# A two-layer decoder trunk: GLA outputs in four parallel banks with one root and one late reciprocal, and gate products in halves between the steps of sliding attention

## The reference, cut to what matters

```
h = rms_norm(x) * (1 + sc1) + sh1
gq, gk, gv, ga, gr, sq, sk, sv, mix_a, mix_b = split(h @ w_in)
y_gla = gla(gq, gk, gv, ga, gr) @ w_up_gla       # 4 heads, dk 64, dv 128, chunks of 64
y_swa = swa(sq, sk, sv) @ w_up_swa               # 8 heads of 64, window 128, 2 kv heads
merged = sigmoid(mix_a) * y_gla + sigmoid(mix_b) * y_swa
# gla, for each chunk n of each head:
#   o = tril(q_dec @ k_inv.T) @ v + q_dec @ state[n];  state[n+1] = decay[n] * state[n] + k_end.T @ v
#   out = o * (mean(o*o) + eps) ** -0.5 * gain * silu(r)
# swa, for each block n of 128 tokens, over blocks n-1 and n:
#   s = q @ k.T / 8, masked; p = exp(s - max) / (sum + exp(sink - max)); o = p @ v
```

## Time and profile before

| | us |
|---|---|
| median of 3 runs | 1620.25 (1618.32 to 1621.02) |
| the profiled execution, its own time | 1614.97 |
| its span (first to last instruction) | 1613.3 |
| PE busy | 1444.3 (90%) |
| DVE busy | 995.4 (62%) |
| ACT busy | 724.7 (45%) |
| POOL busy | 202.8 (13%) |
| mean granted TensorE clock | 0.943 |

### The profile page before, as it was taken

The page is one execution under the profiler, slowest core; times in us unless marked ns, Lnnn a source line. Parts: engine busy times, 40 slices in busy tenths (PEclk is TensorE's granted clock), DMA queues, the critical chain, the costliest instruction groups (busy, mean ns, idle before and its releaser), DMA issues.

```text
span 1613.3 us, 18635 instructions
## 1 busy us (share of the span) xinstructions
PE 1444.3 (90%) x7153; PEld 1140.3 (71%) x7154; DVE 995.4 (62%) x939; ACT 724.7 (45%) x776; POOL 202.8 (13%) x196
## 2 busy tenths in 40 slices
PE   4999967999998899999959997789998899999694
PEld 2766846666677788888748785678877778888472
DVE  2434365341656899999771746444358689999374
ACT  2425134322324677776542432432323567777160
POOL 1000000000001222233210000000002222332111
PEclk9999779999998999999979976999998999999897
DMA  9666200476765899999832210022257499999465
GB/s 304 234 224 237 79 1 6 162 251 224 252 225 199 292 348 391 395 398 398 307 119 104 102 56 0 1 95 73 94 190 271 158 358 380 392 393 392 170 221 188
DMA packets 152802, 350.24 MB, mean 217 GB/s; under 512 B 10511, under 2 KB 12755, under 8 KB 152723
## 3 DMA queue, kind: packets, MB, share of 16 engines
q1 hardware_dynamic: 140018, 312.77, 53.4%
q0 software_dynamic: 12704, 36.38, 6.3%
HBM read 334.43 MB, written 23.61 MB: 222 GB/s over the span
## 4 chain that ended last, share of the span: by engine, by line
PE 74%; DVE 12%; DMA 6%; issue 3%; DVEq 3%; ACT 2%; SPq 1%; POOL 0%; POOLq 0%; ACTq 0%
PE PS L1088 20%; PE PS L1090 19%; PE PS L1089 19%; PE PS L1022 3%; DMA ring<-in_w_ada 2%; DVE ring_parts L1959 2%; PE PS L1388 1%; PE PS L1200 1%; DMA ring<-in_w_down 1%; PE PS L1230 1%; DVEq L1726 1%; PE PS L1017 1%; DVE ring_parts L1605 1%; DVE reg L1766 1%; DVE reg L1746 1%
## 5 line engine op out<-in xcount | busy, mean ns | idle before, releaser
L1089 PE MATMUL PS<-ring_parts,reg_parts 128*128 128x512 f32 x768 | 300.1, 391 | 0.0
L1088 PE MATMUL PS<-ring_parts 128*128 128x512 f32 (+1 forms) x704 | 276.4, 393 | 11.8 <-DVE hT_parts L1613 5.7
L1959 DVE TENSOR_TENSOR ring_parts<-ring,reg_parts 128x2048 fp32r<-128x2048 f32 x124 | 277.9, 2283 | 2.6 <-ACT reg_parts L947 2.6
L947 ACT ACTIVATE reg_parts<-ring 128x2048 fp32r<-128x2048 f32 x124 | 230.4, 1909 | 63.2 <-DMA ring<-in_w_down 36.3
L1605 DVE TENSOR_TENSOR ring_parts<-ring,ring_parts 128x2048 fp32r<-128x2048 f32 (+1 forms) x52 | 112.8, 2210 | 168.3 <-ACT ring_parts L799 168.2
L1088 PE MATMUL PS<-reg_parts 128*128 128x512 f32 x504 | 202.0, 401 | 1.4 <-DVE reg_parts L1987 1.4
L1090 PE MATMUL PS<-reg_parts 128*128 128x512 f32 x504 | 196.9, 391 | 0.0
L1088 PEld LDWEIGHTS PS<-ring_parts 128*128 128x128 f32 x704 | 133.7, 190 | 66.9 <-issue 35.3
L1089 PEld LDWEIGHTS PS<-ring_parts,reg_parts 128*128 128x128 f32 x768 | 145.3, 189 | 28.6
L799 ACT ACTIVATE ring_parts<-ring 128x2048 fp32r<-128x2048 f32 (+1 forms) x52 | 93.3, 1844 | 159.7 <-DMA ring<-in_w_in 125.8
L1959 DVE TENSOR_TENSOR ring_parts<-ring,hT_parts 128x2048 fp32r<-128x2048 f32 x64 | 146.2, 2287 | 14.3 <-issue 13.2
(11 more groups left out here) (316 smaller groups left out, 2137.0 us busy)
## 6 DMA issues: line engine op xcount, KB each, us to landing
ring<-in_w_up SPq DMA_DIRECT2D x32, 2048.0 KB
ring<-in_w_gate SPq DMA_DIRECT2D x32, 2048.0 KB, 11.7
ring<-in_w_down SPq DMA_DIRECT2D x32, 2048.0 KB, 17.9
ring<-in_w_ada SPq DMA_DIRECT2D x40, 1024.0 KB, 5.5
ring<-in_w_in SPq DMA_DIRECT2D x16, 2048.0 KB, 8.1
ring<-in_w_ada SPq DMA_DIRECT2D x4, 2048.0 KB, 16.3
ring<-in_w_out SPq DMA_DIRECT2D x4, 2048.0 KB, 9.2
ring<-in_w_up_gla SPq DMA_DIRECT2D x2, 2048.0 KB
```

What stands on the lines that cost most here:

```text
L947: act.activation(w_high[part][:, cols], ring[:, 3 * k + part, cols], ACT.Copy).then_inc(w_hi[part], 1)
L1088: pe.matmul(out_, left[0], right[0], start=first, stop=False)
L1089: pe.matmul(out_, left[0], right[1], start=False, stop=False)
L1959: tt(ring_r[:, 3 * k + part, cols], ring[:, 3 * k + part, cols], w_high[part][:, cols].bitcast(F32), ALU.subtract).then_inc(w_lo[part], 1)
```

## The change

- `attm` becomes four tiles, one for each head; GpSimd clears the third and fourth, and DVE clears the first two as before. The causal scores come ahead of the chunk states' products, head by head as `r_done` rises. All masked scores are multiplied by v first, each head in its own bank 0 to 3 (the bank of its scores); then the state products follow, with the two heads of a pair taking turns.
- The sums of squares of the four heads are four products with 32 columns of ones into four partition groups of one bank. One root and one reciprocal of 128x512 serve all heads, and a product with one row of ones brings each head's row back to all partitions; DVE multiplies it into `rs` late (`norm_o`). The reciprocal stands on DVE between the scores' scaling of block 1 and the normalising of block 0.
- The transposes of q and k use banks 7, 5, 6, 7 and 5, 6; the scores of block 0 wait for `gate_o` (o times `rs`) only.
- Every gate product of `W_MA0` and `W_MA1` is issued in two halves of four chunks (12 instructions), at the places in the list below. DVE scales the scores of block n + 1, then normalises block n, and only then takes the maximum of n + 1. `split_low(W_MA1)` is taken in two halves, and `split_high(W_UPG)` on ACT comes earlier. GpSimd's router constants wait for the end of the new GLA norm.

The diff, cut; calls that stand alone on a line in the source are joined by semicolons:

```
-        attm = reg5[:, 0:2 * SEQ].rearrange("p (i t s) -> p i t s", i=2, t=NT)
+        attm = reg5[:, :].rearrange("p (h t s) -> p h t s", h=GH, t=NT)
-        osq = [reg0[:, 512 * h:512 * h + 512] for h in range(GH)]
-        orr = [reg7[:, 512 * i:512 * i + 512] for i in range(2)]
+        osq = [reg23[:, 512 * h:512 * h + 512] for h in range(GH)]
+        o_inv = reg7[:, 512:1024]
...
+    pool.wait_ge(b_done, at(b_done, l, 1))
+    pool.memset(attm[:, 2, :, :], 0.0).then_inc(scanm_made, 1)
+    if l == 0:
+        pool.wait_ge(ada_ready, 2)
+    pool.memset(attm[:, 3, :, :], 0.0).then_inc(scanm_made, 1)
...
+    act.activation(warm[:, :], one, ACT.Sqrt)
...
+    square_o(0); square_o(1); copy_qT(0); square_o(2); square_o(3)
+    act.wait_ge(ms_ready, at(ms_ready, l, 1))
+    act.activation(o_inv, PS[:, 4, :], ACT.Sqrt, scale=1.0 / P, bias=eps).then_inc(orr_done, 1)
+    for t in range(1, NT):
+        copy_qT(t)
...
+        copy_probs(3, b)
+    split_high(W_UPG)
+    act.wait_ge(o_done, at(o_done, l, 2 * GH + 1))
     act.activation(rs_parts[0].rearrange("p h s -> p (h s)"), reg4[:, :], ACT.Copy).then_inc(out_hi, 1)
+    copy_o(3)
...
+    for h in range(GH):
+        rows = slice(HD * (h % 2), HD * (h % 2) + HD)
+        pe.wait_ge(r_done, at(r_done, l, h + 1))
+        if h == 0:
+            pe.wait_ge(const_loaded, 16 * 9)
+        for t in range(NT):
+            mm = pe.matmul(PS[:, h, t * P:t * P + P], kinv[rows, h // 2, t * P:t * P + P],
+                           qdec[rows, h // 2, t * P:t * P + P], start=True, stop=True)
+        mm.then_inc(att_ready, 1)
+    pe.wait_ge(kt_done, at(kt_done, l, 2))
+    if l == 0:
         pe.wait_ge(ada_added, 2)
...
+        pe.wait_ge(att_done, at(att_done, l, h + 1))
+            pe.matmul(PS[:, h, t * P:t * P + P], v[:, t, h * P:h * P + P], attm[:, h, t, :],
+    pe.wait_ge(s_done, at(s_done, l, 1))
+    for m in range(2):
+            for h in (2 * m, 2 * m + 1):
+                rows = slice(HD * (h % 2), HD * (h % 2) + HD)
+                mm = pe.matmul(PS[:, h, n * CHUNK:n * CHUNK + CHUNK], S[rows, m, n, :],
+                               qdec[rows, m, n * CHUNK:n * CHUNK + CHUNK], start=False, stop=(n == NCH - 1),
+                               skip_group_check=True)
+                if n == NCH - 1:
+                    mm.then_inc(o_ready, 1)
+    pe.wait_ge(rope_done, at(rope_done, l, 1))
+    def transpose_q(t):
+        for a in range(QH // 2):
+            mm = pe.transpose(PS[:, QT_BANKS[t], a * P:a * P + P], qk[:, t, 2 * a:2 * a + 2, :].rearrange("p h d -> p (h d)"), ident[:, :])
+        mm.then_inc(qT_ready, 1)
+    for i in range(NT // 2):
+        for t in (2 * i, 2 * i + 1):
+            for g in range(KVH):
+                o = ((t % 2) * KVH + g) * P
+                mm = pe.transpose(PS[:, 5 + i, o:o + P], kd[:, t, g, :, :].rearrange("p r d -> p (r d)"), ident[:, :])
+        mm.then_inc(kT_ready, 1)
+    transpose_q(0)
+        mm = pe.matmul(PS[32 * h:32 * h + 32, 4, :], ones[:, 0:32], osq[h], start=True, stop=True, skip_group_check=True)
+    mm.then_inc(ms_ready, 1)
+    pe.wait_ge(kT_done, at(kT_done, l, 1))
+    transpose_q(1)
+    pe.wait_ge(kT_done, at(kT_done, l, 2))
+    transpose_q(2)
+    pe.wait_ge(qT_done, at(qT_done, l, 1))
+    transpose_q(3)
+    pe.wait_ge(o_done, at(o_done, l, GH))
...
+    def gate_half(bank, unit, j, part):
+        w = parts(unit)
+        for k in range(4 * part, 4 * part + 4):
+            mm = three_passes(PS[:, bank, :], [a[:, k, j * P:j * P + P] for a in w], [a[:, k, :] for a in hT_parts],
+                              k == 0, k == C - 1)
+        if part == 1:
+            mm.then_inc(mx_ready, 1)
+    def early_gate(n, part):
+        if part == 0:
+            if n == 0:
+                wait_unit(W_MA0)
+                pe.wait_ge(qT_done, at(qT_done, l, 2))
+            else:
+                pe.wait_ge(early_done, at(early_done, l, n))
+        gate_half(5, W_MA0, n, part)
+    def late_gate(j, part):
+        if j == 0 and part == 0:
+            wait_unit(W_MA1)
+            pe.wait_ge(sc_read, at(sc_read, l, NT))
+        elif j >= 2 and part == 0:
+            pe.wait_ge(o_done, at(o_done, l, INVERTED + j + 1))
+        gate_half(mix_bank(Q_MA1 + j), W_MA1, j, part)
...
+    def inverse_rows(h):
+        if h == 0:
+            pe.wait_ge(o_done, at(o_done, l, INVERTED))
+            pe.wait_ge(sc_read, at(sc_read, l, NT))
+        elif h >= 2:
+            pe.wait_ge(o_done, at(o_done, l, INVERTED + h - 1))
+        pe.matmul(PS[:, 2 + h % 2, :], ones[32 * h:32 * h + 1, :], o_inv[32 * h:32 * h + 1, :], start=True, stop=True).then_inc(ms_ready, 1)
 
...
+    scores(0); early_gate(0, 0); scores(1); early_gate(0, 1); transpose_probs(0, 1); early_gate(1, 0); values(0)
+    scores(2); early_gate(1, 1); transpose_probs(1, 0); transpose_probs(1, 1); early_gate(2, 0); values(1); scores(3)
+    early_gate(2, 1); transpose_probs(2, 0); transpose_probs(2, 1); early_gate(3, 0); values(2); early_gate(3, 1)
+    inverse_rows(0); inverse_rows(1); late_gate(0, 0); transpose_probs(3, 0); transpose_probs(3, 1); inverse_rows(2)
+    inverse_rows(3); late_gate(0, 1); values(3); late_gate(1, 0); late_gate(1, 1); next_half(0); late_gate(2, 0)
+    late_gate(2, 1); next_half(1); late_gate(3, 0); next_half(2); late_gate(3, 1); next_half(3)
...
+    split_low(W_MA1, parts_=(0,))
+    def gate_o(h):
+        tt(rs[:, h, :], PS[:, h, :], rs[:, h, :], ALU.mult).then_inc(o_done, 1)
+    def copy_kT(i):
+        dve.wait_ge(kT_ready, at(kT_ready, l, i + 1))
+        dve.tensor_copy(kT[:, :, 2 * P * i:2 * P * i + 2 * P].rearrange("p g (t s) -> p t g s", s=P),
+                        PS[:, 5 + i, :].rearrange("p (t g s) -> p t g s", t=2, g=KVH)).then_inc(kT_done, 1)
+    gate_o(0); gate_o(1); copy_kT(0); copy_kT(1); gate_o(2); gate_o(3)
...
+    def norm_o(h):
+        dve.wait_ge(ms_ready, at(ms_ready, l, h + 2))
+        tt(rs[:, h, :], PS[:, 2 + h % 2, :], rs[:, h, :], ALU.mult).then_inc(o_done, 1)
+    scale_scores(0); score_max(0)
+    dve.wait_ge(orr_done, at(orr_done, l, 1))
+    scale_scores(1)
+    dve.reciprocal(o_inv, o_inv).then_inc(o_done, 1)
+    normalise(0); score_max(1); copy_probs(0, 1); scale_scores(2); normalise(1); score_max(2); copy_probs(1, 0)
+    copy_probs(1, 1); scale_scores(3); normalise(2); score_max(3); copy_probs(2, 0); copy_probs(2, 1)
+    split_low(W_MA1, parts_=(1,))
+    normalise(3); norm_o(0); norm_o(1); copy_probs(3, 0); copy_probs(3, 1); norm_o(2); norm_o(3)
```

More of the change, by code:

```diff
@@ L1273, in next_half @@
                         condition_half(l + 1, j)
-                pe.wait_ge(pv_done, at(pv_done, l, NT))
-                wait_unit(W_MA1)
-                for j in range(C // 2):
-                    channel_major(mix_bank(Q_MA1 + j), W_MA1, slice(j * P, j * P + P)).then_inc(mx_ready, 1)
-                    next_half(j)
+                scores(0)
+                early_gate(0, 0)
+                scores(1)
+                early_gate(0, 1)
+                transpose_probs(0, 1)
+                early_gate(1, 0)
+                values(0)
+                scores(2)
+                early_gate(1, 1)
+                transpose_probs(1, 0)
+                transpose_probs(1, 1)
+                early_gate(2, 0)
+                values(1)
+                scores(3)
+                early_gate(2, 1)
+                transpose_probs(2, 0)
+                transpose_probs(2, 1)
+                early_gate(3, 0)
+                values(2)
+                early_gate(3, 1)
+                inverse_rows(0)
+                inverse_rows(1)
+                late_gate(0, 0)
+                transpose_probs(3, 0)
+                transpose_probs(3, 1)
+                inverse_rows(2)
+                inverse_rows(3)
+                late_gate(0, 1)
+                values(3)
+                late_gate(1, 0)
+                late_gate(1, 1)
+                next_half(0)
+                late_gate(2, 0)
+                late_gate(2, 1)
+                next_half(1)
+                late_gate(3, 0)
+                next_half(2)
+                late_gate(3, 1)
+                next_half(3)
                 wait_unit(W_UPG)
@@ L1590, in _ @@
                     scale_tokens(t, t + 1)
-                dve.memset(attm[:, :, :, :], 0.0)
+                dve.memset(attm[:, 0:2, :, :], 0.0)
                 if l == 0:
@@ L1597, in _, with split_low @@
                     second_scale()
-                def split_low(n, l=l):
-                    for h in range(2):
+                def split_low(n, l=l, parts_=(0, 1)):
+                    for h in parts_:
                         cols = slice(half_split[n] * h, half_split[n] * (h + 1))
@@ L1694, in _ @@
                     second_scale().then_inc(ada_added, 1)
-                def mask_scores(h):
+                for h in range(GH):
                     dve.wait_ge(att_ready, at(att_ready, l, h + 1))
-                    if h >= 2:
```

(12 more changed lines are left out.)

193 lines of the change are left out of this document (98 added, 95 removed).

## The result

The changed kernel takes 1550.7 us (median of 4 runs, 1549.0 to 1555.2) against 1619.3 (4 runs, 1617.6 to 1621.0): ratio 0.9581, 95% interval 0.9558 to 0.9604. In its profiled execution it took 1555.17 us, 59.8 less than the profiled one of before.

A forecast was written before the change was run, and what follows sets the result against it. PE's work, clock and waits were taken to bound the kernel. A saves 51.0 us and B costs 5.4, so 45.6 off the profiled 1614.97 gives 1569.4; with 5.3 to the median, forecast 1574, range 1554 to 1596.

The forecast's parts named there:

- Stretch A: Each layer, end of `W_R` products to scores of block 0: forecast 25.0 and 24.0 us, from 50.4 and 49.6.
- Causal scores, states and two transposes: Start of A: scores 2.5 us while filling PE's wait for the last `r_done`, state products and transposes 3.6; sum 6.1.
- `att @ v`: In A, four heads in a row, 4.6 to 8.0 us, taken as 5.6; as cover for DVE's states 0.3 short.
- State products: In A, two heads taking turns on the two row halves: 3.7 us, bounds 3.2 and 13.
- Transposes, squares, sums, changes of shape: Rest of A: first transposes 2.2 us, squares and sums 3.0, last q transposes 2.4, tile shape changes 1.0.
- everything at the full clock: Lower bound of A: 19.5 us if PE ran all of it at the full clock.
- Stretch B: Each layer, scores of block 0 to first `W_UPG` product: forecast 2.7 us longer, 88.0 against 85.3 without clock loss.
- The waits: PE's waits in B: forecast 15.3 us, against 15.6 before, so they hardly shrink.
- The new wait for DVE's copy: B, blocks 1 and 2: second transposes wait for DVE's copy, now behind the maximum; 2.3 us each.
- The loss by the clock: In B, time lost to the low clock, left unchanged at 6.5 us in layer 0 and 4.1 in layer 1.
- clock stays up: Rival: A takes 19.5 us and B loses its low-clock cost; 20 us more saved, 1554; chance 0.22.
- the two rivals in which the low clock spreads over gate halves: B: six more halves per layer at low clock, 1603 us, chance 0.1; or all 32 halves, 1641, chance 0.03.

The follow-up runs named there:

- the control: The changed kernel run again unaltered, against the kernel before: median 1554.4 us, ratio 0.9599.
- the late reciprocal's run: Changed kernel with the one reciprocal moved behind the copy of block 0's probabilities: median 1540.8 us, ratio 0.9512 against the kernel before.
- the run with heads apart: Changed kernel with a pair's state products issued one head after the other, not in turn: median 1561.0 us, ratio 0.9637 against the kernel before.
- the run with each head's products together: Changed kernel with each head's `att @ v` followed by its own state products: median 1586.2 us, ratio 0.9784 against the kernel before.

## Why the prediction was wrong

The direction was right, and the time was 23.3 us too high. Of these, 14.2 lie in the sum (1569.4 against the profiled 1555.17), 4.5 in that this execution lay above its kernel's median, and 4.6 in the step from the profiled execution of before to the median. The 14.2 come from both stretches in like parts: A was 8.1 shorter than forecast in the two layers and B 8.5, less 2.4 outside of both.

Two steps failed: the clock in A, of which the prediction held that part of it stays low, and the waits in B.

**Stretch A, the clock.** Forecast 25.0 and 24.0, measured 21.7 and 19.2 (19.2 and 19.2 in the control). Term by term in layer 1:

- Causal scores, states and two transposes: 6.1 forecast, 5.2 measured (914.67 to 919.91). The 3.26 for the chunk states was read from a row that ran at a mean clock of 0.66; at the full one they take 2.25.
- `att @ v`: 5.6, and 5.1 with the wait for the states (3.84 + 1.24). That these products are a little short as cover was seen, but as 0.3 and not 1.24.
- State products: 3.7, and 3.34.
- Transposes, squares, sums, changes of shape (2.2 + 3.0 + 2.4 + 1.0 = 8.6): 5.6 measured (928.32 to 933.89). Here the prediction took durations between the two clocks, and there was only the full one.

The bound "everything at the full clock", 19.5, was the right value, up to one low stretch of 2.5 us in some executions, and the rival that has it got 0.22. I argued against it from B's waits, where I should have asked of A alone what stood there before the clock fell. The experiments give the ladder of A in layer 1, from one execution each: 49.6 before; 36.1 with one root and reciprocal, the new banks and nothing in A that waits for a reciprocal, but each head's products in the old order; 25.1 with `att @ v` of all heads ahead of all state products; 19.2 with heads taking turns. The last two steps, 16.9, are the order of products that PE did before too. Of these, 2.7 are the longer wait, 2.9 the two halves at once, and the rest is clock, which the wait and the single heads brought together.

**Stretch B, the waits.** Forecast 2.7 more in each layer, measured 2.0 and 1.1 less. Three terms of it were too large. The waits: 15.3 forecast, 12.2 idle measured (88.3 less 76.1). The one for block 0's probabilities is 4.56 (forecast 4.8), the next two 2.44 (2.7): right. The new wait for DVE's copy was priced at 2.3 twice and is 1.3 and 0.8: this is the wait that was mis-sized, 4.6 against 2.1. The products with a row of ones: 2.3, forecast 3.0. PE's work itself: 71.1 at the full clock by the late reciprocal's run, forecast 72.7. The loss by the clock, left as it was at 6.5 and 4.1, is 5.4 (81.4 less 76.0) and 5.0 (76.1 less 71.1): about right in sum. So the rival "clock stays up" is right in A but for one low stretch in layer 0, and wrong in B, and the two rivals in which the low clock spreads over gate halves are refuted.

**The point I had not priced** is that the wait of 4.56 us which the reciprocal makes costs more in clock than in idle time. Moving it gave 13.6 us for 6.7 of instructions; in the profiled executions B's idle time fell by 3.2 in the two layers and PE's busy time by 11.0.

**The offset.** I added 4.6 us to get from one execution to the median, and the profiled execution of the changed kernel then lay on the other side of its own. The kernel before took 1614.0 us at a mean clock of 0.944 and 1624.8 at 0.936 among 27 runs, so a single profile can't place a sum better than some 5 us either way; a range that ends 20 us below a forecast of 45 saved was narrow for that and the clock together.

## What to carry to other kernels

Where small products stand in a stretch at the low clock, don't carry that clock over to a new order: work out the stretch at both clocks, and take the full one if what stood there before the fall (a wait, single heads on half of the rows) is gone, with one low stretch (here 2.5 us) as the margin. Put products that use different rows in turn, and gather the independent ones ahead of those that wait. A slow vector instruction (3.35 us) belongs where its engine idles, and a reordering is judged by PE's busy time with the same work as well as by its waits.

## What the runs showed of the hardware

The clock stood at 0.50 over 18.8 us in which PE was busy 18.72, with products on 64 rows one after another, as before; in the run with heads apart it fell while such products ran, with the same 1.24 us wait ahead of them as in the control, where it did not. With the heads in turn it fell there too, but in 4 stretches of 18. A busy PE by the profile is thus no guarantee of the full clock. Ahead of other falls PE was idle: within the waits of 4.56 us in B, and at the end of the 3.91 us in the run with each head's products together. How long the clock then stayed at 0.50 differs by what followed: 24 us with single heads, up to 7 with transposes and gate products. The same work costs PE 71.1 or 76.1 us (B of layer 1), by low stretches that lie at different places in different executions.
